# Decoder trunk with eight experts: another order of the first expert steps

## What is computed

```python
def moe_ffn(x, w_router, wg, wu, wd):
    xt = x.reshape(B * S, D)
    logits = (xt @ w_router).astype(jnp.float32)
    top_v, top_i = lax.top_k(logits, TOP_K)
    w = jax.nn.softmax(top_v, axis=-1)
    gates = jnp.sum(jax.nn.one_hot(top_i, N_EXPERTS, dtype=jnp.float32) * w[..., None], axis=1)
    for e in range(N_EXPERTS):
        y = y + gates[:, e:e + 1].astype(xt.dtype) * swiglu(xt, wg[e], wu[e], wd[e])
```

## Time and profile before

| | |
|---|---|
| median of three runs | 1472.94 us (1471.33 to 1474.48) |
| the profiled execution | 1472.44 us |
| its span | 1470.7 us |
| TensorE busy | 1396.2 us, 95% |
| VectorE busy | 819.5 us, 56% |
| ScalarE busy | 705.5 us, 48% |
| DMA, mean over the span | 302 GB/s |
| DMA from 600 to 1444 us | 405 GB/s |

### The profile page before, as it was taken

How to read it: one execution, slowest core, us unless ns; L and a number is a source line. 1 busy time by engine, 2 the same in 40 slices (tenths; PEclk the granted TensorE clock), 3 DMA queues, 4 the chain that set the end, 5 groups by cost and what they waited for, 6 DMA issues and landing times.

```text
span 1470.7 us, 16634 instructions
## 1 busy us (share of the span) xinstructions
PE 1396.2 (95%) x6613; PEld 1012.9 (69%) x6613; DVE 819.5 (56%) x794; ACT 705.5 (48%) x773; POOL 35.9 (2%) x92
## 2 busy tenths in 40 slices
PE   8989999999899897999999999999999999999995
PEld 6865688888777746675756785757667757666574
DVE  4624454544354246655647675756656846547476
ACT  5454443444253523445635564545446645436363
POOL 2000000000000000000000000000000000000011
PEclk9989999999999897999999999999999999999998
DMA  9630755555343224999999999999999999999993
GB/s 342 224 115 1 258 199 180 192 174 176 137 148 126 104 86 158 410 409 409 402 409 410 403 393 394 409 411 409 409 396 410 410 409 403 409 410 409 402 403 128
DMA packets 148478, 444.37 MB, mean 302 GB/s; under 512 B 9454, under 2 KB 21612, under 8 KB 148396
## 3 DMA queue, kind: packets, MB, share of 16 engines
q1 hardware_dynamic: 146836, 438.24, 77.8%
q0 software_dynamic: 1440, 4.98, 0.8%
q10 hardware_dynamic: 120, 0.04, 0.0%
HBM read 439.30 MB, written 3.93 MB: 301 GB/s over the span
## 4 chain that ended last, share of the span: by engine, by line
PE 86%; DVE 5%; ACT 4%; DMA 2%; issue 1%; POOL 0%; DVEq 0%; POOLq 0%; SPq 0%; ACTq 0%
PE bank L821 83%; PE bank L824 3%; DVE ring_l L1772 1%; ACT part_h L1394 1%; DMA most<-in_moe_w_down_dram 1%; DMA ring<-in_moe_w_down_dram 1%; DVE most_l L1772 1%; DVE part_l L1772 0%; DVE more_l L1772 0%; ACT junk L1403 0%; ACT xh L1394 0%; ACT prob L1595 0%; DVE y L1772 0%; ACT probT L1394 0%; DVE gm L1777 0%
## 5 line engine op out<-in xcount | busy, mean ns | idle before, releaser
L1394 ACT ACTIVATE part_h<-ring 128x2048 fp32r<-128x2048 f32 x144 | 274.1, 1918 | 136.9 <-PE bank L821 132.4
L821 PE MATMUL bank<-part_h,xh 128*128 128x512 f32 x784 | 312.1, 398 | 6.1 <-DVE xl L2180 2.5
L821 PE MATMUL bank<-part_h,xl 128*128 128x512 f32 x784 | 306.2, 391 | 0.0
L1772 DVE TENSOR_TENSOR ring_l<-ring,part_h 128x2048 fp32r<-128x2048 f32 x102 | 231.6, 2289 | 49.5 <-ACT part_h L1394 48.7
L821 PEld LDWEIGHTS bank<-part_h,xh 128*128 128x128 f32 x784 | 147.6, 188 | 46.9 <-issue 8.2
L821 PE MATMUL bank<-part_h,hTh 128*128 128x512 f32 x392 | 156.2, 398 | 17.0 <-DVE ring_l L1772 10.2
L821 PEld LDWEIGHTS bank<-part_h,xl 128*128 128x128 f32 x784 | 147.5, 188 | 31.7
L821 PE MATMUL bank<-part_h,hTl 128*128 128x512 f32 x392 | 153.9, 393 | 0.0
L1772 DVE TENSOR_TENSOR part_l<-ring,part_h 128x2048 fp32r<-128x2048 f32 x42 | 96.1, 2292 | 83.8 <-ACT part_h L1394 83.8
L1772 DVE TENSOR_TENSOR part_l<-part_in,part_h 128x2048 fp32r<-128x2048 f32 x54 | 123.0, 2289 | 32.6 <-ACT part_h L1394 32.1
L821 PE MATMUL bank<-part_l,xh 128*128 128x512 f32 x360 | 140.2, 389 | 0.0
(11 more groups left out here) (320 smaller groups left out, 1837.9 us busy)
## 6 DMA issues: line engine op xcount, KB each, us to landing
ring<-in_moe_w_down_dram SPq DMA_DIRECT2D x60, 1024.0 KB, 13.9
ring<-in_moe_w_up_dram SPq DMA_DIRECT2D x58, 1024.0 KB, 14.7
ring<-in_moe_w_gate_dram SPq DMA_DIRECT2D x50, 1024.0 KB, 12.6
part_in<-in_moe_w_down_dram SPq DMA_DIRECT2D x36, 1024.0 KB, 14.0
most<-in_moe_w_gate_dram SPq DMA_DIRECT2D x27, 1024.0 KB, 14.8
part_in<-in_moe_w_up_dram SPq DMA_DIRECT2D x27, 1024.0 KB, 13.4
part_in<-in_moe_w_gate_dram SPq DMA_DIRECT2D x21, 1024.0 KB, 15.2
most<-in_moe_w_up_dram SPq DMA_DIRECT2D x17, 1024.0 KB, 13.2
```

The lines of the kernel that those rows point to most:

```text
L821: return nc.tensor.matmul(o, lhsT, rhs, start=start, stop=stop)
L1394: return nc.scalar.activation(dst, src, ACT.Copy, scale=scale)
L1772: return nc.vector.tensor_tensor(o, a, b, op)
```

## The change

The first eight letters of the list of steps change from `WNWNWWNW` to `WWNWNWNW`. Steps 0 and 1 are now chunks 0 and 1 of place 0, step 2 is the first of place 1, and steps 1 to 5 are wide, narrow, wide, narrow, wide; from step 6 on all is as before. The gather of place 2 has to stand in a narrow step and moves from step 3 to step 4, and the slot matrices of place 3, which share a buffer with it, follow.

```diff
     STEPS = [(narrow_steps if kind == "N" else wide_steps).pop(0)
-             for kind in "WNWNWWNW" "WNWNWWNW" "WNWNWWNW" "WNWNWNWW"]
+             for kind in "WWNWNWNW" "WNWNWWNW" "WNWNWWNW" "WNWNWNWW"]
...
-        GATHER_STEP = {1: 0, 2: 3, 3: 6, 4: 9, 5: 14, 6: 19, 7: 22}
+        GATHER_STEP = {1: 0, 2: 4, 3: 6, 4: 9, 5: 14, 6: 19, 7: 22}
...
-        SLOTS_AT = {MOE_AT[0, 0, 1]: 1, MOE_AT[0, 1, 3]: 2, last_piece(1, 3): 3, last_piece(1, 6): 4,
+        SLOTS_AT = {MOE_AT[0, 0, 1]: 1, MOE_AT[0, 1, 3]: 2, last_piece(1, 4): 3, last_piece(1, 6): 4,
```

## The result

The changed kernel takes 1477.68 us in the median of 20 runs, the kernel before 1473.23 in 20 runs: ratio 1.0028 [1.0021, 1.0036], or 4.1 us slower. The forecast was 1476.0, which is 3.1 us slower. One of the 20 runs of the changed kernel was a slow one of 2846.95 us; it is left out of the ratio, and nothing here explains it.

What follows compares the result with a forecast made beforehand. Loads and TensorE bound the expert stage side by side; which waits decides. Loads 2.3 us late at load 32, 3.1 from the thin place: +3.1 on 1472.44 is 1475.5, plus 0.5 to the median, 1476.0; range 1470.5 to 1479.0.

Steps and rivals of the forecast that it cites:

- The early loads: Loads 8 to 11 follow pieces 5 to 7 at once, not at 579.97 us: 10.2 us of loading in idle time.
- The vector engine's detours: In steps 0 and 1, now both wide, vector work before splits makes TensorE wait 5.0 us in sum.
- The two small terms: Taken off the 5.0 us of waits, 0.4 and 0.1 leave TensorE 4.5 us later at the end of step 5.
- When load 32 lands: Load 32 follows TensorE's piece 20 by 5.1 us, landing at 650.1 against 647.8: loads 2.3 us late.
- its best case: Without any TensorE wait, load 32 would land at 645.8, held by its predecessors: 2.0 us earlier than before.
- The thin place: Near 881 us the backlog is only 1.4 us; TensorE 4.5 us late makes the loads 3.1 late, not 2.3.
- Down to the end: At 1331 us TensorE's 1.4 us wait absorbs lateness beyond the loads'; the end is 3.1 us late.
- the slow clock: After the 3.3 us wait at 1384 TensorE's clock falls to 1.2 GHz for 3.4 us; forecast to stay.
- The detours found no cover: Rival, 25%: the vector engine's detours find cover, and the end is 1.8 us earlier, 1471.1, or 1469.6 without the slow clock.
- The thin queue costs more: Rival, 20%: an empty queue near 881 us loses another 2 to 2.5 us, giving 1478.2.
- The early loads did come: Rival, 3%, said they don't: something else holds pieces 8 to 11 until 580 us; the time is the same 1476.

Runs made afterwards that it cites:

- e2: The changed kernel with the loads of pieces 8 to 11 held back until the expert order is known; 1478.65 us, ratio 1.0032 to the kernel before.
- e7: The changed kernel with slots(3), slots(4) and slots(6) moved between narrow pieces; 1476.33 us, ratio 1.0024 to the kernel before.
- e9: The kernel before, with SyncE waiting before load 8 until TensorE has used pieces 0 and 1; 1475.77 us, ratio 1.0019.
- e1: The changed kernel with token_rows and slots(2) moved from wide step 1 to narrow step 2; 1475.55 us, ratio 1.0005 to the kernel before.
- e3: The kernel before with token_rows alone moved from narrow step 1 to wide step 2; 1478.36 us, ratio 1.0033.
- e4: The kernel before with the ten instructions giving the expert order placed ahead of place 0's low rows; 1474.19 us, ratio 1.0002.
- e6: The kernel before with both the earlier expert order and slots(3), slots(4), slots(6) between narrow pieces; 1471.76 us, ratio 0.9981.
- e5: The kernel before with slots(3), slots(4) and slots(6) moved between narrow pieces; 1472.83 us, ratio 0.999.

## Why the forecast came out

**The early loads.** Right. They were issued from 558.93 on (by 560, the forecast said). The forecast kept 2.0 of their 10.2 us at best and nothing once the detours are counted; e2 shows no gain from them that can be measured.

**The vector engine's detours.** Right in place and in sum. TensorE's timeline of after, the four waits:

```profile
606.09 0.39 PE L821 MATMUL bank<-part_h,xl 128*128 128x512 f32 x1
606.90 0.50 PE L821 MATMUL bank<-part_h,xh 128*128 128x512 f32 x1 [0.43 <-DVE ring_l L1772]
...
610.30 0.66 PE L824 MATMUL bank<-ident,y 128*128 128x128 f32 x4 [0.39 <-DVE y L1772]
...
621.51 0.51 PE L821 MATMUL bank<-part_h,xh 128*128 128x512 f32 x1 [1.87 <-DVE ring_l L1772]
...
628.35 0.51 PE L821 MATMUL bank<-part_h,xh 128*128 128x512 f32 x1 [0.99 <-DVE more_l L1772]
```

The forecast had 0.5, 0.9, 1.9, 0.3 and 1.4. The wait of 0.3 is not there, and 0.9 and 1.4 show as 0.4 and 1.0. But a recorded gap is less than what is lost. In a running stream these matmuls start 0.23 us apart; across the first gap the starts lie 0.81 apart (606.09 and 606.90), so 0.58 us are lost where the gap says 0.43. Counted from the use of one piece to the use of the next, with 2.72 us for a wide piece and 0.5 for each of the two turns, the five places lose 0.7, 0.6, 2.2, 0.1 and 1.3 us, and 0.2 go before piece 18: 5.1 us, where the forecast had 5.0. Piece 19 is used at 645.2 and piece 20 at 647.1, the forecast's 643.1 and 645.0 shifted by 2.1, of which 1.9 lie ahead of the stage. The vector engine's timeline shows the detour behind the largest:

```profile
613.43 2.29 DVE L1772 TENSOR_TENSOR ring_l<-ring,part_h 128x2048 fp32r<-128x2048 f32 x1 [0.39 <-ACT part_h L1394]
615.64 0.17 DVE L1776 TENSOR_SCALAR stays<-place 128x8 f32<-128x8 f32 x1
...
619.17 2.28 DVE L1772 TENSOR_TENSOR ring_l<-ring,part_h 128x2048 fp32r<-128x2048 f32 x1
```

Between two splits stand the 3.5 us of `token_rows` that begin with `stays`. The split that TensorE needs starts at 619.17, and TensorE goes on at 621.51. Late at the end of step 5: 4.5 us, forecast 4.5. The two small terms that led there from 5.0 (0.4 and 0.1) had no row behind them.

**When load 32 lands.** This term was mis-sized. The forecast put it at the use of piece 20 plus 5.1 us, the row of a load issued into an idle queue. Load 32 took 6.7 us, and the loads are 4.1 us late and not 2.3. It found a queue: load 31 landed at 651.33 and load 32 at 653.84, 2.5 us behind. Of the 1.8 us, 0.7 follow from the forecast's own numbers. Piece 20 is narrow, so load 32 goes out only 1.9 us after load 31 (645.25 and 647.13), and at 2.56 us of data each it has to wait for it. In its best case the forecast counted this hold by the predecessors, in its sum it left it out. Another 1.0 comes from load 30, which landed 6.4 us after its issue at 642.53 though its queue was empty, and held the two behind it:

```profile
part_in<-in_moe_w_down_dram SPq DMA_DIRECT2D x1, 1024.0 KB, 6.4
```

The last 0.1 to 0.2 are TensorE's. Besides the weight loads, the DMA engines had one packet of another queue from 646 to 649 us, at 646.84:

```profile
q8 instruction: 1, 0.02, 2.0%
```

Nine of the loads of after from 12 to 32 that found an empty queue took 4.8 to 5.1 us (16 to 20, 26 to 29). Four landed late by themselves: 12 (5.9 us), 21 (7.6), 24 (6.3) and 30 (6.4). From 583 to 650 us there are three packets of this queue, at 587.7, 614.6 and 646.8, and each starts while load 12, 21 or 30 is under way; load 24 has none. In e2 and e7 load 30 has such a packet too and takes 6.1 and 6.3 us. That the packet causes the delay is likely, but no run tests it. The Trainium skill, "DMA: Bandwidth & Descriptors", section "Anatomy of one DMA", would have 4.4 us for 1 MiB (for transfers that GpSimd issues); the shortest of loads 12 to 32 here took 4.8 us, nearer to the row's 5.1.

**The thin place.** Wrong, because the loads come to it later than forecast. The forecast let the loads arrive there 2.3 us late and leave 3.1 late. They arrive 4.4 late, as late as TensorE, so the queue stays about as it was (load 124 goes out at 887.57, a backlog of 1.2 us, where the earlier trace rows had 1.4). Load 123:

```profile
884.52 0.37 SPq L703 DMA_DIRECT2D most<-in_moe_w_up_dram  x1
```

```profile
most<-in_moe_w_up_dram SPq DMA_DIRECT2D x1, 1024.0 KB, 6.8
```

It lands at 891.29 and load 124 at 893.84, 2.55 us later, where the kernel before has 3.76. So the thin place costs nothing further. It even takes 1.2 us off the lateness, because the delay that the kernel before has there does not occur: the loads are 3.2 late behind it.

**Down to the end.** Partly wrong. From load 124 to 312 the lateness grew again from 3.2 to 4.5 us, where the forecast let it stand. With loads as late as TensorE, 1331 absorbs nothing: the waits are 1.09 and 3.36 us in place of 1.37 and 3.29.

```profile
1337.85 0.50 PE L821 MATMUL bank<-part_h,hTh 128*128 128x512 f32 x1 [1.09 <-DVE most_l L1772]
...
1390.77 0.50 PE L821 MATMUL bank<-part_h,hTh 128*128 128x512 f32 x1 [3.36 <-DVE ring_l L1772]
```

That the waits and the slow clock stay was forecast, and e9 shows the premise, that the loads set the end. The sum is 4.1 instead of 3.1 us. The mis-sized term alone is 1.8 us too low, and the thin place, which was to add 0.8, adds nothing. Load 32 is 4.1 us late and the ratio at the end is 4.1 us as well, but that is in part luck: in between the loads gained 1.2 us at the thin place and lost 1.4 behind it, and neither was forecast.

**The rivals.** The detours found no cover (e1 gives back 3.4 us once they are moved). "The thin queue costs more" named the wrong place: loads 12 to 32 of after, issued into a nearly empty queue, took 5.8 us in the mean and not 5.1, but what counted was load 32 at 647 us, not the place at 881, which cost less than before. The early loads did come.

**Open.** In after, e3, e2 and e9 the lateness or lead of the loads drifts by 0.2 to 1.7 us between load 124 and load 312, also in e4. Landings there lie 2.56 us apart, except at 7 to 12 places in each trace with 2.9 to 4.6 us, which are not the same in every kernel. Over the eleven traces these are 104 landings, and at 96 of them a packet of an instruction queue or of GpSimd's own transfers starts between 1 us before the predecessor's landing and the load's own; among the other 1975 landings that is so at 333. So such packets go with most of the late landings, but no run removes them, and most landings beside such a packet are on time. Why the places add up to more in after, e2, e3 and e4 (1.4 to 1.7 us) than in e9 (0.2) is not settled, and neither is their share of the +4.1 us.

## What to carry over

Where loads and TensorE are equally busy, follow the two lags separately through the ring of buffers: a lag of TensorE reaches the loads only where their queue is empty, a lag of the loads reaches TensorE only where it waits for them, and in between each is invisible. A gain on one side alone fades at the first place where the other decides (e4). Moving both together was the fastest here (e6), though its interval overlaps with that of the better edit alone (e5). Before reordering steps, look at what small vector instructions are bound to them by position: here 5.4 us of such work (3.55 and 1.84) moved from between narrow pieces to between wide ones decided the result, and the 10.2 us of early loading did not. And when a load goes out into a queue that was just empty, look at its predecessor before taking the idle price.

## What had not been expected of the hardware

**The clock can fall after a short wait, and below 2 us its length does not tell.** In e3 2.3 us of waiting (TensorE was busy for 2.66 of 5 us) were followed by 3.4 us at 1.2 GHz, a loss of 2.0 us on top. From 600 to 1440 us every wait of 2.3 us or more, in all eleven traces, was followed or accompanied by such a stretch. In e5 it was the one of 4.9 us at 1331:

```profile
1334.40:1335.20 0.80, 0.80 (x3) 0.62 (x2) 0.80 (x1) 0.80 (x1) 0.00 (x0) 0.50 1.04 415
```

Of the 48 waits of 1.77 to 1.87 us, 45 were not followed by one and three were. In after the wait of 1.87 us at 621 was not, one of 1.77 us at 987.6 was; in e7 the wait of 1.86 us at 618.7, at the same place of the program as the one at 621, was as well (after first, then e7):

```profile
989.20:992.60 3.40, 3.40 (x10) 2.66 (x9) 3.29 (x11) 0.65 (x1) 0.00 (x0) 0.51 1.03 410
```

```profile
620.10:623.50 3.40, 3.40 (x10) 2.63 (x9) 3.29 (x10) 0.38 (x1) 0.00 (x0) 0.50 0.39 161
```

What a slow stretch costs depends on what comes next. In e3 at 646 nothing covered it, and the clock nearly doubled what the wait had cost. At the other three places TensorE would have waited about 1 us for a split right behind it; that wait is gone, and TensorE is only 0.2 us later than without the slow stretch.

**A load of 1 MiB into a nearly empty queue varies.** With an empty queue ahead and no late landing it took 4.8 to 5.1 us. One after another at 2.72 us, in after, the loads took 4.8 to 7.6 us, although each had more time than the 2.56 us of its data. The longer ones stood behind a late predecessor or, as told above for loads 12, 21 and 30, had a packet of an instruction queue beside them; load 24 had neither. A single delay of 1.3 us then travels through the loads behind it, since each of them gives back only 0.16 us.
